# Differential attention's head norm with tokens on partitions, in a two-block fp32 kernel

## The reference

```python
def diff_maps(q, k, v, lam):                       # 4 heads, 512 queries, 768 keys, head width 128
    s = jnp.einsum("bhmqd,bhmkd->bhmqk", q, k) * (DIFF_DH ** -0.5)
    a = jax.nn.softmax(s, axis=-1)
    w = a[:, :, 0] - lam * a[:, :, 1]
    return jnp.einsum("bhqk,bhkd->bhqd", w, v)

def diff_out(o, subln_g, lam_init):                # rmsnorm over the 128 values of a head
    o = rmsnorm(o, subln_g) * (1.0 - lam_init)
    return o.transpose(0, 2, 1, 3).reshape(B, L, H * VD)
...
    x = x + g_a * (jnp.concatenate([attn_x, hyo_x], axis=-1) @ p["w_out"])
```

## Time and profile before

| | |
|---|---|
| median of 3 runs | 1477.31 us (1476.94 to 1478.07) |
| the profiled execution, its span | 1475.7 us |
| PE busy | 1452.9 us, 98% of the span |
| DVE, ACT, POOL busy | 820.2, 615.2, 320.4 us |
| instructions | 17703 |

### The profile page before, as it was taken

How to read it: one execution, slowest core, us unless ns; L and a number is a source line. 1 busy time by engine, 2 the same in 40 slices (tenths; PEclk the granted TensorE clock), 3 DMA queues, 4 the chain that set the end, 5 groups by cost and what they waited for, 6 DMA issues and landing times.

```text
span 1475.7 us, 17703 instructions
## 1 busy us (share of the span) xinstructions
PE 1452.9 (98%) x6988; PEld 1189.8 (81%) x6988; DVE 820.2 (56%) x1216; ACT 615.2 (42%) x968; POOL 320.4 (22%) x289
## 2 busy tenths in 40 slices
PE   9999999999999999999999999999999999999998
PEld 7776778888878888888888878877788888888887
DVE  6455766444566543654457447777757444345434
ACT  6544772223454322343354336564435333223332
POOL 1362220102032100121025312136531111111102
PEclk9999999999999999999999999999999999999999
DMA  8351116545264444365327221235513333323321
GB/s 272 112 176 52 58 44 235 193 157 185 72 228 151 163 160 152 117 213 186 115 99 261 71 79 51 72 110 171 183 65 115 100 101 100 100 86 101 100 86 57
DMA packets 54605, 189.94 MB, mean 129 GB/s; under 512 B 6584, under 2 KB 7385, under 8 KB 54395
## 3 DMA queue, kind: packets, MB, share of 16 engines
q1 hardware_dynamic: 48442, 167.06, 34.6%
q0 software_dynamic: 4880, 17.30, 3.5%
q10 hardware_dynamic: 1200, 4.46, 0.8%
HBM read 176.20 MB, written 12.60 MB: 128 GB/s over the span
## 4 chain that ended last, share of the span: by engine, by line
PE 91%; DVE 4%; ACT 3%; issue 1%; DMA 0%; POOL 0%; SPq 0%; DVEq 0%; ACTq 0%; POOLq 0%
PE PS L481 90%; PE PS L494 2%; DVE TMP L2300 1%; ACT wh L1188 0%; DVE TMP L1849 0%; DMA X<-in_x 0%; DVE wl L1801 0%; DVE HTl L2383 0%; ACT TMP L1706 0%; ACT HTh L1210 0%; DVE HTl L1817 0%; ACT HTh L1699 0%; DVE TMP L1842 0%; ACT Y L1202 0%; ACT TMP L1285 0%
## 5 line engine op out<-in xcount | busy, mean ns | idle before, releaser
L1801 DVE TENSOR_TENSOR wl<-raw,wh 128x1024 fp32r<-128x1024 f32 x208 | 271.3, 1308 | 316.6 <-ACT wh L1188 316.4
L481 PE MATMUL PS<-HTh,wh 128*128 128x512 f32 (+1 forms) x1072 | 418.2, 391 | 4.5 <-DVE TMP L1875 1.9
L481 PE MATMUL PS<-HTl,wh 128*128 128x512 f32 (+1 forms) x1072 | 414.7, 387 | 0.0
L481 PE MATMUL PS<-HTh,wl 128*128 128x512 f32 (+1 forms) x1072 | 411.7, 387 | 0.0
L1188 ACT ACTIVATE wh<-raw 128x1024 fp32r<-128x1024 f32 x228 | 239.3, 1053 | 272.7 <-PE PS L481 268.3
L481 PEld LDWEIGHTS PS<-HTh,wh 128*128 128x128 f32 x1072 | 201.6, 188 | 52.2 <-issue 7.6
L481 PEld LDWEIGHTS PS<-HTh,wl 128*128 128x128 f32 x1072 | 200.7, 188 | 41.3
L481 PEld LDWEIGHTS PS<-HTl,wh 128*128 128x128 f32 x1072 | 201.7, 188 | 39.0 <-DVE HTl L1817 0.7
L481 PE MATMUL PS<-wh,FFh 128*128 128x512 f32 (+1 forms) x442 | 170.2, 385 | 0.0
L481 PE MATMUL PS<-wh,FFl 128*128 128x512 f32 (+1 forms) x442 | 169.9, 384 | 0.0
L481 PE MATMUL PS<-wl,FFh 128*128 128x512 f32 (+1 forms) x442 | 169.9, 384 | 0.0
(11 more groups left out here) (339 smaller groups left out, 2078.5 us busy)
## 6 DMA issues: line engine op xcount, KB each, us to landing
raw<-in_ws SPq DMA_DIRECT2D x268, 512.0 KB, 3.8
taps<-TMP SPq DMA_DIRECT2D x16, 256.0 KB, 2.5
tab<-in_spec POOLq DMA_DIRECT2D x8, 512.0 KB, 5.1
raw<-taps SPq DMA_DIRECT2D x8, 512.0 KB, 3.6
kd<-TMP POOLq DMA_DIRECT2D x16, 256.0 KB, 6.4
wh<-in_wd POOLq DMA_DIRECT2D x8, 512.0 KB, 4.0
wl<-in_wd POOLq DMA_DIRECT2D x8, 512.0 KB, 4.7
kf<-kd SPq DMA_DIRECT2D x8, 512.0 KB, 3.8
```

The costliest lines, as they stand in the source:

```text
L481: return nc.tensor.matmul(out, l, r, start=start, stop=stop, skip_group_check=True)
L1801: tt(WL[k][:, :n], RAW[RAW_AT["unit", u, 0] % RAWS][:, :n], f32(WH[k][:, :n]), ALU.subtract).then_inc(sem("lo_dve"), 1)
```

## The change

The values of a pair come out transposed, with tokens on partitions and the head's 128 values along the row: the two operands of the six matmuls in `diff_values` trade places. DVE copies the result to one tile, `XO`. ACT squares each block of it with a running sum along the row, which gives the column of sums at once. `sub_sums` and its bank are gone. The factors are made as before, and ACT multiplies each block of `XO` by its column of factors in place (`sub_scaled`). PE transposes the four blocks of a head (`sub_turn`) at the places where `sub_scale` stood. ACT makes `O2h` from PSUM with the gain, and DVE, no longer POOL, makes `O2l` from PSUM and `O2h`. ACT loads the table of the square root by an instruction of its own behind the last square. Line numbers past L481 differ by some units between the two kernels.

```diff
...

-                    i = mm(PS[:, b, 256:384], V2[:, k, h * P:(h + 1) * P], WT[n % 2][:, k, :], k == 0, k == 5)
+                    i = mm(PS[:, b, 256:384], WT[n % 2][:, k, :], V2[:, k, h * P:(h + 1) * P], k == 0, k == 5)
...
-            def sub_sums():
-                b = bank("sub", "sub_v", 1, ACC)
...
-            def sub_scale(h):
-                b = bank(("sn", h), "sn_v", h + 1, RING4 if h == 1 else ACC)
-                e.wait_ge("sn_dg", 4 * h + 4)
-                mm(PS[:, b, :], ONES, NDG[:, :], True, True).then_inc(sem("p_sn"), 1)
+            def sub_turn(h):
+                b = bank(("sn", h), "o2_lo", h + 1, RING4 if h == 1 else ACC)
+                e.wait_ge("sn_x", 4 * h + 4)
+                for i in range(4):
+                    r = tp(PS[:, b, i * P:(i + 1) * P], XO[:, i, h * P:(h + 1) * P])
+                r.then_inc(sem("p_sn"), 1)
...
...
-            def diff_values(n):
-                e.wait_ge("p_dv", n + 1)
-                act(O2F[:, h, qb * P:(qb + 1) * P], PS[:, BANK["dv", n], 256:384], ACT.Copy,
-                    scale=SUBG).then_inc(sem("dv_o"), 1)
-            def diff_squares(h):
-                e.wait_ge("dv_ev", 4 * h + 4)
-                act(S2F[:, h, :], S2F[:, h, :], ACT.Square, scale=2.0 ** -4).then_inc(sem("s2_sq"), 1)
+            def diff_squares(n):
+                e.wait_ge("dv_ev", n + 1)
+                act(SQO[:, :], XO[:, qb, h * P:(h + 1) * P], ACT.Square, scale=2.0 ** -4,
+                    accum_out=SUBR[:, n:n + 1]).then_inc(sem("s2_sq"), 1)
...
+            diff_squares(len(DIFF) - 1)
+            tables("sqrt_and_others")
+            def sub_scaled(h):
+                e.wait_ge("sub_v", 7)
+                for i in range(4):
+                    x = XO[:, i, h * P:(h + 1) * P]
+                    act(x, x, ACT.Copy, scale=SUBR[:, 32 + 4 * h + i:33 + 4 * h + i]).then_inc(sem("sn_x"), 1)
             def sub_high(h):
-                e.wait_ge("sn_v", h + 1)
-                act(O2h[:, h, :], NO2[:, :], ACT.Copy).then_inc(sem("o2_hi"), 1)
+                e.wait_ge("p_sn", h + 1)
+                e.wait_ge("lam_v", 6)
+                act(O2h[:, h, :], PS[:, BANK["sn", h], :], ACT.Copy, scale=SUBG).then_inc(sem("o2_hi"), 1)
...
...
-                e.wait_ge("dv_o", n + 1)
-                ts(S2F[:, h, qb * P:(qb + 1) * P], PS[:, BANK["dv", n], 256:384], 2.0 ** 64, -2.0 ** 64, ALU.min,
-                   ALU.max).then_inc(sem("dv_ev"), 1)
+                e.wait_ge("p_dv", n + 1)
+                nc.vector.tensor_copy(XO[:, qb, h * P:(h + 1) * P], PS[:, BANK["dv", n], 256:384]).then_inc(sem("dv_ev"), 1)
...
-            def sub_high(h):
-                tt(NO2[:, :], O2F[:, h, :], PS[:, BANK["sn", h], :], ALU.mult).then_inc(sem("sn_v"), 1)
+            def sub_low(h):
+                e.wait_ge("o2_hi", h + 1)
+                stt(O2l[:, h, :], PS[:, BANK["sn", h], :], SUBG, f32(O2h[:, h, :]), ALU.mult,
+                    ALU.subtract).then_inc(sem("o2_lo"), 1)
...
...
-            def sub_low(h):
-                tt(O2l[:, h, :], NO2[:, :], f32(O2h[:, h, :]), ALU.subtract).then_inc(sem("o2_lo"), 1)
```

More of the change, by code:

```diff
@@ L306, in program @@
         QTh, QTl = at("QTh", 120, [P, 4, S], F32R), at("QTl", 144, [P, 4, S], F32R)
-        O2h, O2l = at("O2h", 136, [P, 4, S], F32R), at("O2l", 144, [P, 4, S], F32R)
-        O2F, S2F = at("o2f", 136, [P, 4, S]), at("s2f", 128, [P, 4, S])
+        O2h, O2l = at("O2h", 128, [P, 4, S], F32R), at("O2l", 144, [P, 4, S], F32R)
+        XO, SQO = at("xo", 136, [P, 4, S]), at("sqo", 128, [P, P])
         V2 = at("V2", 152, [P, 6, S])
@@ L1074, in tensor_program @@
                     forward(o, f)
-                    if f == 0 and o == 0:
-                        sub_sums()
                     if f == 1 - o:
-                        sub_scale(3 * o)
+                        sub_turn(3 * o)
                     if f == 3 and o == 0:
-                        sub_scale(1)
+                        sub_turn(1)
                     if f == 1 and o:
@@ L1097, in tensor_program @@
                     hyena_group(10)
-                    sub_scale(2)
+                    sub_turn(2)
             def wide2(n, banks, parts):
@@ L1588, in scalar_program @@
                 if n > 1:
-                    diff_values(n - 2)
+                    diff_squares(n - 2)
                 if n == len(DIFF):
@@ L1597, in scalar_program @@
                     diff_scores(n, 1)
-                    if n > 1 and n % 4 == 1:
-                        diff_squares((n - 5) // 4)
                     if n % 2:
@@ L1647, in scalar_program @@
                         if o == 0:
-                            sub_diag(1)
+                            sub_scaled(1)
                     if f == 3 and o == 0:
                         sub_high(1)
-                        sub_diag(2)
+                        sub_scaled(2)
                     if f == 1 and o:
@@ L1670, in scalar_program @@
                     sub_high(2)
-                    sub_diag(3)
+                    sub_scaled(3)
                     conv_center(10)
@@ L2306, in vector_program @@
             spectral(0)
-            ps, fits, r, q = PS[:, BANK["sub"], 0:16], SUBR[:, 0:16], SUBR[:, 16:32], SUBR[:, 32:48]
-            e.wait_ge("p_sub", 1)
-            tt(q, ps, R0, ALU.mult).then_inc(sem("sub_v"), 1)
+            sums, r, q = SUBR[:, 0:16], SUBR[:, 16:32], SUBR[:, 32:48]
+            e.wait_ge("s2_sq", 16)
+            tt(q, sums, R0, ALU.mult).then_inc(sem("sub_v"), 1)
             e.wait_ge("sub_v", 1)
@@ L2313, in vector_program @@
             e.wait_ge("sub_v", 2)
-            ts(fits, q, 2.0 ** 100, 0.0625, ALU.is_lt, ALU.mult).then_inc(sem("sub_v"), 1)
+            ts(sums, q, 2.0 ** 100, 0.0625, ALU.is_lt, ALU.mult).then_inc(sem("sub_v"), 1)
             ts(r, q, 2.0 ** 100, 2.0 ** 21, ALU.min, ALU.mult).then_inc(sem("sub_v"), 1)
@@ L2319, in vector_program @@
             e.wait_ge("sub_v", 5)
-            tt(q, q, fits, ALU.mult).then_inc(sem("sub_v"), 1)
+            tt(q, q, sums, ALU.mult).then_inc(sem("sub_v"), 1)
             e.wait_ge("sub_v", 6)
@@ L2329, in vector_program @@
                     if f == 1:
-                        sub_high(3 * o)
+                        sub_low(3 * o)
                     if f == 1 and o:
@@ L2333, in vector_program @@
                     if f == 3 and o == 0:
-                        sub_high(1)
+                        sub_low(1)
                 hyena_conv(8 + 3 * o)
@@ L2349, in vector_program @@
                         fold_low(1, c)
-                    sub_high(2)
+                    sub_low(2)
                     hyena_conv(9)
@@ L2672, in gpsimd_program @@
                            ALU.subtract).then_inc(sem("ys_lo"), 1)
-                    if f == 1:
-                        sub_low(3 * o)
-                    if n == 3:
-                        sub_low(1)
                     if f >= 2:
@@ L2686, in gpsimd_program @@
                     weights(unit("w_in_2", 0, 1536 + 10 * P) + SLOTS - 1)
-                    sub_low(2)
             weights(unit("w_out_2", 3 * P, 0) + SLOTS - 1)
```

25 lines of the change are left out of this document (4 added, 21 removed).

## The result

| | us |
|---|---|
| before, median of 20 runs | 1477.09 |
| changed, median of 20 runs (1478.88 to 1481.57) | 1480.11 |
| ratio, 95% interval | 1.0024 (1.0018 to 1.0030) |
| span of the changed kernel's profiled execution, whose own time is 1481.21 | 1479.5 |

Two of the twenty runs of the kernel before were slow (1613 and 1810 us) and are not in the ratio; without them its median is 1477.05. The ratio compares the two sets of runs and is not the quotient of the medians: it comes to 3.5 us where the medians differ by 3.0, and the two spans by 3.8. The interval of the ratio leaves out 1, so the changed kernel is slower, by 0.2%.

What follows compares the result with a forecast made beforehand. PE, busy 98% of the span, was taken as the bound. Terms 0.07 - 0.3 + 1.7 - 0.42 + 1.75 = +2.8 us took 1477.31 to 1480.1; range 1477.7 to 1482.9, the forecast's own 1479.2 to 1481.2.

Steps and rivals of the forecast that it cites:

- the two places: PE's waits ahead of the first transposes (6 to 7 us) and in backward(1, 0) (1.7 to 2 us).
- the line that the prediction drew at 1480.3: Median above which the kernel would count as slower; about 0.2%, 3 us, can be told from no change.
- The attention loop: Squares replace copies under ACT's idle time: no change in the loop, about 0.07 us at its end.
- The first factors: Before head 0's transposes: sums hidden beside spectral(0), factors 0.1 us later, transposes 0.42 cheaper; together -0.3 us.
- The clock: Behind PE's wait for the first factors: half clock on the path, +1.7 us, bounds 0 and 2.05.
- Head 1: Transposes in place of the product by ones: another 0.42 us less for PE.
- Heads 2 and 3, and the bank: Round 1: DVE late, second accumulator waits for hyena_conv(10) in a shifted bank; +1.75 us, bounds -0.3 and +2.6.
- The full clock: Rival: clock stays full when PE resumes after the first wait; 1478.4 us, chance 0.12.
- miss each other: Rival: POOL's wl starts behind DVE's instruction in the first factors' chain, up to 1.9 us shorter; 1476.5 us, chance 0.07.
- One more POOL instruction: Rival: POOL gets ahead at the start of DVE's factor chain, which waits 1.28 us more; 1481.4 us, chance 0.07.
- The second half-clock stretch: Rival: PE's rests at round 1's accumulators drop the clock again, another 1.7 us; 1481.8 us, chance 0.25.

Runs made afterwards that it cites:

- e5_no_sums: The kernel before without the sixteen one-column products, its factors made from other numbers (wrong results): 1478.27 us, ratio 1.0014.
- e3_fill: The changed kernel with 26 needless 512-column matmuls in PE's first wait, behind forward(0, 1): 1478.88 us, ratio 1.0016.
- e1_bank: The changed kernel with the ring ACC of accumulator banks moved one bank on: 1479.48 us, ratio 1.0017.
- e6_pool: The changed kernel with POOL's low parts of spectral(0) ahead of the weight unit: 1481.10 us, ratio 1.0029.
- e4_chain: The changed kernel with DVE's factors, and ACT's root and first scaling, ahead of spectral(0): 1477.77 us, ratio 1.0009.
- e10: The changed kernel with the edits of both e1_bank and e3_fill: 1477.54 us, ratio 1.0002.
- e11: The changed kernel with only the loads of the filter spectra of stages 2 and 3 ahead of the weight units: 1479.38 us, ratio 1.0019.
- e12: e9 with the weight unit again ahead of the rounding and low parts of spectral(0) on ACT and POOL: 1472.91 us, ratio 0.9975.
- e2: The kernel before with the ring ACC set back by one behind sub_sums, giving later users the changed kernel's banks: 1477.20 us, ratio 1.0006.
- e7: The changed kernel with factors first, POOL's order and banks rearranged, and heads 0, 2 and 3 handled earlier: 1478.50 us, ratio 1.0015.
- e8: e7 with SyncE issuing the filter spectra of stages 2 and 3 ahead of the weight unit: 1471.93 us, ratio 0.9967.
- e9: e8 with head 1's four transposes behind backward(0, 1) and not ahead of it: 1471.65 us, ratio 0.9966.

## Why the prediction was right

The time (1480.11 against 1480.1), the mechanism and the two places were right. By the line that the prediction drew at 1480.3 the result counts as "the same", to which it gave 0.43, against 0.54 for slower; the interval of the ratio shows that it is slower by a little. By the steps:

- **The attention loop: nothing.** `forward(0, 0)` ends at 978.30, before at 978.29. The squares took 0.32 us and 0.19 for the read of the sum, 0.38 and 0.1 were put in.
- **The first factors.** The sums were hidden, as `e5_no_sums` shows by itself. L2284 ended at 983.01, and was put at 983.03. PE resumed 0.31 us later than before, and about 0.1 was forecast (987.65; the 987.53 given there for before is 987.56 in the earlier trace rows): the chain's last but one step took 0.51 beside POOL's low part, where before it took 0.18. Transposes for the product by ones: 0.43 by `e3_fill`, 0.42 forecast.
- **The clock: the term that was mis-sized.** 2.31 us and not 1.7. Both rows that the term was taken from show a stretch of 3.4 us; here it was 6.6, and 4.7 of it lay behind the resumption. My upper bound of 2.05 took its end from the same rows and was too low.
- **Head 1.** The lead over before goes from +2.19 us at `backward(0, 0)` to +1.80 at head 2's transposes: 0.39 gained, 0.42 forecast.
- **Heads 2 and 3, and the bank.** From +1.80 to +3.71 at the second accumulator is 1.91 us, against 1.75. L2284 is no longer held (0.68 us, before 1.92), and the two waits for `spectral` are 0.30 and 0.81 us, 1.1 in place of about 1.8. The wait for the convolution is 1.47 us, under the 1.7 to 2 that the prediction named. ACT's rounding took 0.67 and DVE's low part 0.75, each 0.05 more than put in. The bank makes 1.5 of this by `e1_bank`.
- **The sum** by the profiles is 0.31 - 0.43 + 2.31 - 0.39 + 1.91 = 3.7, and another 0.1 by the output projection (1059.12 against 1055.27). The forecast was 2.8, and the medians gave 3.0; the profiled span was put at 1478.5 and is 1479.5. So the hit is in part luck, closer than the terms deserve: in the profiled executions the clock cost 0.6 more than forecast, and the whole is 0.8 larger in the two spans than in the medians. How much the clock costs differs between executions (below).
- **The rivals.** The full clock is out (0.50 for 6.6 us). POOL's `wl` had begun 0.8 us ahead of L2284, as forecast, so the two didn't miss each other; `e6_pool` made them miss there, and lost it again at the chain's end, against the subtraction that had been put off. One more POOL instruction did get in the way, but at L2302 and for 0.34 us, not at the chain's start for 1.28. The second half-clock stretch isn't in the changed kernel's profile; in `e4_chain` it is, behind the same wait. It may differ between executions of the changed kernel too; no run shows that.

The Trainium skill, TensorE: Matmul & The Clock Gate (HAM oscillation), says that waits which let the gate close are paid by the work behind them; the trace agrees, with 5.57 us against 3.26 for the same matmuls. The Trainium skill, TensorE: Matmul & The Clock Gate (Part 1: The HAM clock gate), says that the number of slow matmuls varies from run to run of one kernel. Each kernel here has one profile, so no trace shows it for one kernel; profiles of different kernels differ so at 136 us, in a stretch that the edits don't touch (last section).

## What to carry to other kernels

Work that runs while a chain on other engines is the bound is free, and it may be holding the clock loss where it hurts nobody; before taking it out, look at what PE waits for behind it, and shorten that first. Each removed allocation from a ring of banks shifts all later ones: read off which bank the next accumulator falls into. When a chain is moved earlier, follow it through every queue it depends on, the DMA queue included, for the gain is lost at the first load that was just in time: here 7.8 us were won and lost again until one load was issued ahead of another.

## What the runs showed of the hardware

**The clock's fall after a short wait differs between executions.** At about 135 us PE waits for 1.91 or 1.92 us in every one of the fourteen profiled kernels, in a part that no edit touches. In eight of them (the kernel before, the changed one, `e3`, `e5`, `e6`, `e10`, `e11`, `e12`) the clock fell to 0.50 for a stretch at about the end of that wait, and in the other six (`e1`, `e2`, `e4`, `e7`, `e8`, `e9`) it stayed 1.00. Here are `e1_bank`'s wait and a stretch behind it, beside the last row:

```profile
134.75 0.50 PE L480 MATMUL PS<-HTh,wh 128*128 128x512 f32 x1 [1.91 <-DVE TMP L1860]
```

```profile
136.00:139.40 3.40, 3.33 (x20) 2.46 (x19) 1.80 (x2) 2.85 (x6) 1.33 (x2) 1.00 0.00 0
```

The times go with it. The changed kernel's 20 runs fall into ten of 1478.9 to 1479.8 and ten of 1480.5 to 1481.6, and the kernel before shows two groups about as far apart (1475.6 to 1476.3, and 1476.9 to 1478.3). The profiled executions with the stretch are of an upper group (changed kernel, 1481.21; `e6_pool`, 1481.10 beside 1479.13), and most of those without it lie low among the runs of their kernel (`e1_bank`, 1477.37 beside 1479.66); `e4_chain`'s, 1479.67 and high, has its second stretch at 1039 us instead. That this stretch makes the two groups is likely by this, but not shown, as no kernel was profiled in both. A median can therefore move by a microsecond with the share of each group, and single terms under 1 us are better read from stretches of the trace than from ratios.

The waits of over 6 us were followed by half clock in every profile that has one (6.28, 6.36, 6.66, 6.76 and 7.32 us). Those of 1.47 to 1.92 us went either way: the 1.53 and 1.80 in the two fastest kernels were followed by none. Those of 2.15 (`e12_weights_first`) and 3.14 us (`e4_chain`), seen once each, were followed by it.

**A small VectorE instruction can be held for the whole of a GpSimd one.** A 128x16 step takes 0.16 to 0.29 us when POOL is idle, and took 0.51, 1.13 and 2.26 when it began while one of POOL's subtractions ran. The Trainium skill, SBUF — State Buffer (the shared port pair), describes this as an exclusive lock which the later instruction waits for in full. The trace agrees: L2304 in `e6_pool` began at 984.98 and ended at 987.24, and POOL's subtraction ended at 987.21.
